# Two blocks on one core: the input's rows at 512 columns, and the working region 64 bytes further on

## What is computed

```python
x = first_block(x, meta_tokens, ...)     # 16 meta tokens ahead of the 512: 528 rows, dropped again at its end
    # h += W_out(recurrent heads + latent attention), squared-ReLU MLP of 4096
    # then a causal pooling layer and a second such MLP
return second_block(x, mem_2, ...)       # 512 rows
    # u = rms_norm(h); u @ gdn_w_in; gated delta rule, attention over 256 memory rows; @ w_out
    # f = swiglu(rms_norm(h), w_ffn_in, w_ffn_out), hidden width 2816
```

## Time and profile before

| | |
|---|---|
| time, median of three runs | 1871.85 us (1867.13 to 1872.07) |
| span of the profiled execution, first to last instruction | 1864.1 us |
| the profiled execution's own time | not given apart; one of the three |
| median less the span | 7.7 us |
| TensorE busy, mean granted clock | 1822.0 us (98%), 0.997 |
| VectorE, ScalarE busy | 1309.2 us (70%), 925.2 us (50%) |
| DMA | 162.55 MB, 87 GB/s |

### The profile page before, as it was taken

How to read it: one execution, slowest core, us unless ns; L and a number is a source line. 1 busy time by engine, 2 the same in 40 slices (tenths; PEclk the granted TensorE clock), 3 DMA queues, 4 the chain that set the end, 5 groups by cost and what they waited for, 6 DMA issues and landing times.

```text
span 1864.1 us, 31132 instructions
## 1 busy us (share of the span) xinstructions
PE 1822.0 (98%) x12498; PEld 1661.9 (89%) x12498; DVE 1309.2 (70%) x1882; ACT 925.2 (50%) x1557; POOL 33.4 (2%) x31
## 2 busy tenths in 40 slices
PE   7999999999999999999999999999999999999997
PEld 7888878999999999898899877787889898999996
DVE  4664476767777775877777768678738379877775
ACT  5456454544343446654344433645567464544453
POOL 0110001100000000000000000000000000000000
PEclk9999999999999999999999999999999999999999
DMA  5211101222233232333233322222200422333331
GB/s 197 70 57 58 60 1 46 81 102 91 91 106 99 80 119 91 102 102 103 91 111 103 103 92 91 80 68 79 80 1 27 144 80 91 114 102 102 107 109 57
DMA packets 63364, 162.55 MB, mean 87 GB/s; under 512 B 4632, under 2 KB 29464, under 8 KB 63096
## 3 DMA queue, kind: packets, MB, share of 16 engines
q1 hardware_dynamic: 62368, 158.59, 25.7%
q10 hardware_dynamic: 856, 2.00, 0.3%
HBM read 156.38 MB, written 4.19 MB: 86 GB/s over the span
## 4 chain that ended last, share of the span: by engine, by line
PE 89%; DVE 5%; ACT 3%; DMA 1%; issue 1%; DVEq 1%; ACTq 0%; SPq 0%
PE ps L714 76%; PE ps L1389 2%; DMA ULF<-W 1%; PE ps L929 1%; PE ps L1409 1%; PE ps L1258 1%; DVE wlo L3379 1%; PE ps L1394 0%; PE ps L1235 0%; PE ps L1237 0%; PE ps L904 0%; ACT WU L2620 0%; DVE wlo L3009 0%; PE ps L905 0%; PE ps L1521 0%
## 5 line engine op out<-in xcount | busy, mean ns | idle before, releaser
L714 PE MATMUL ps<-UH,whi 128*128 128x264 f32 (+2 forms) x1280 | 413.0, 323 | 11.2 <-DVE wlo L3009 10.4
L714 PE MATMUL ps<-UL,whi 128*128 128x264 f32 (+2 forms) x1280 | 403.0, 315 | 0.0
L714 PE MATMUL ps<-UH,wlo 128*128 128x264 f32 (+3 forms) x992 | 288.5, 291 | 0.0
L714 PEld LDWEIGHTS ps<-UH,whi 128*128 128x128 f32 x1280 | 241.4, 189 | 30.3 <-issue 13.6
L714 PEld LDWEIGHTS ps<-UL,whi 128*128 128x128 f32 x1280 | 241.4, 189 | 17.6 <-issue 2.4
L714 PEld LDWEIGHTS ps<-UH,wlo 128*128 128x128 f32 (+1 forms) x992 | 186.9, 188 | 2.7
L1947 ACT ACTIVATE whi<-raw 128x1024 fp32r<-128x1024 f32 x114 | 119.3, 1052 | 83.9 <-PE ps L714 63.2
L714 PE MATMUL ps<-KFH,whi 128*128 128x264 f32 x512 | 145.7, 285 | 1.6 <-DVE KFL L3421 1.5
L714 PE MATMUL ps<-KFH,wlo 128*128 128x264 f32 x512 | 145.3, 284 | 0.0
L714 PE MATMUL ps<-KFL,whi 128*128 128x264 f32 x512 | 145.2, 284 | 0.0
L714 PE MATMUL ps<-TH,whi 128*128 128x256 f32 x504 | 139.1, 276 | 0.0
(11 more groups left out here) (577 smaller groups left out, 4552.8 us busy)
## 6 DMA issues: line engine op xcount, KB each, us to landing
raw<-W SPq DMA_DIRECT2D x134, 512.0 KB, 3.5
raw_p<-W SPq DMA_DIRECT2D x46, 1024.0 KB, 4.9
ULF<-W SPq DMA_DIRECT2D x44, 512.0 KB, 4.0
raw_d<-W SPq DMA_DIRECT2D x14, 512.0 KB, 3.9
H<-xT SPq DMA_DIRECT2D x4, 528.0 KB, 7.5
spill<-H SPq DMA_DIRECT2D x1, 2048.0 KB, 7.0
H<-spill SPq DMA_DIRECT2D x1, 2048.0 KB, 8.4
MEM<-memT ACTq DMA_DIRECT2D x1, 1024.0 KB, 4.8
```

What stands on the lines that cost most here:

```text
L714: mm = pe.matmul(dst, a, b, start=start and n == 0, stop=stop_ and n == 2, skip_group_check=again)
```

## The change

Two things move, and no instruction is added, removed or reordered, nor any wait.

- The stages that use 512 tokens get an input of their own, USH and USL, [128, 8, 512] each, placed inside UH's and UL's room at u_at + 384 = 82944, which is 81 x 1024. USL lies 16384 bytes behind USH. Every row of both begins at 0 modulo 1024. The DMA target for the second MLP's down pieces and the place of its snapshots are cut out of the same room with rows of 2048 bytes instead of 2112.
- S0 moves from 134080 to 134144, which is 131 x 1024; the rows that began at 960 modulo 1024 begin at 0. The first MLP's KFH and KFL move by 64 bytes too. OMH, MH, ML, KTH, KTL, the first MLP's UH and UL, and the weights stay.

```diff
@@ -177,7 +177,8 @@  (Space)
-    parts: list
+    inputs: object
+    inputs_lo: object
@@ -292,6 +293,8 @@  (build)
         UH = place("UH", [P, KT, L], FR)
         UL = place("UL", [P, KT, L], FR)
+        us_at = u_at + 384
+        assert us_at + 2 * KT * SEQ * 4 <= u_at + 2 * KT * L * 4
@@ -303,7 +306,7 @@
-        S0 = base[0]
+        S0 = base[0] + 64
@@ -443,12 +446,14 @@
+        USH, USL = region(us_at, ("USH", [P, KT, SEQ], FR), ("USL", [P, KT, SEQ], FR))
+        USF, USLF = region(us_at, ("USF", [P, KT, SEQ], F32), ("USLF", [P, KT, SEQ], F32))
...
         space0 = Space(L, HALF, [KFH0, KFH1], [KFL0, KFL1], [KG_0, KG_1], KTH, KTL, KX, KFO, UF[:, 0:4, HALF:L],
-                       ULF[:, 0:4, HALF:HALF + 2 * P], [slice(0, HALF), slice(HALF, L)], R2[:, :], R[1][:, :], ((7, 5, 6), (4, 5, 6)))
-        space1 = Space(SEQ, NMEM, [MFH0, MFH1], [MFL0, MFL1], [GM0, GM1], MTH, MTL, XT, FOM, UF[:, 0:4, META + NMEM:L],
-                       ULF[:, 0:4, META + NMEM:L], [slice(META, META + NMEM), slice(META + NMEM, L)], R2[:, META:L], R[1][:, META:L],
+                       ULF[:, 0:4, HALF:HALF + 2 * P], UH, UL, R2[:, :], R[1][:, :], ((7, 5, 6), (4, 5, 6)))
+        space1 = Space(SEQ, NMEM, [MFH0, MFH1], [MFL0, MFL1], [GM0, GM1], MTH, MTL, XT, FOM, USF[:, 0:4, NMEM:SEQ],
+                       USLF[:, 0:4, NMEM:SEQ], USH, USL, R2[:, META:L], R[1][:, META:L],
                        ((7, 1, 3), (4, 5, 6)))
@@ perceptron, mlp_pair
-                    return UH[:, k, h.parts[0]]
+                    return h.inputs[:, k, 0:h.half]
...
-                    half_product(z, v + 2, 1, lambda k: UH[:, 4 + k, h.parts[1]], lambda k: UL[:, 4 + k, h.parts[1]], False)
+                    half_product(z, v + 2, 1, lambda k: h.inputs[:, 4 + k, h.half:h.tokens],
+                                 lambda k: h.inputs_lo[:, 4 + k, h.half:h.tokens], False)
...
-                    tile(KT, h.tokens, lambda k: u(order[k]), lambda k: ul(order[k]), before=split_input(m) if j == 0 else None)
+                    tile(KT, h.tokens, lambda k: h.inputs[:, order[k], :], lambda k: h.inputs_lo[:, order[k], :],
+                         before=split_input(m) if j == 0 else None)
@@ the gate columns and the 36 gin tiles
-                mm = passes(ps[0:16, 7, :], ABH[:, k, :], ABL[:, k, :], tok(u(k), SEQ), tok(ul(k), SEQ), k == 0,
+                mm = passes(ps[0:16, 7, :], ABH[:, k, :], ABL[:, k, :], us(k), usl(k), k == 0,
...
-                tile(KT, SEQ, u, ul, before=between(j))
+                tile(KT, SEQ, us, usl, before=between(j))
@@ the first tiles of the last MLP, in halves and whole
-                        mm = passes(ps[:, 2 * (t % 2) + e // 2, x * NMEM:(x + 1) * NMEM], wh, wl, UH[:, k, part(x)],
-                                    UL[:, k, part(x)], k == 0, k == KT - 1)
+                        mm = passes(ps[:, 2 * (t % 2) + e // 2, x * NMEM:(x + 1) * NMEM], wh, wl, us(k)[:, half(x)],
+                                    usl(k)[:, half(x)], k == 0, k == KT - 1)
...
-                    mm = passes(ps[:, bank, :], wh, wl, UH[:, k, META:L], UL[:, k, META:L], k == 0, k == KT - 1)
+                    mm = passes(ps[:, bank, :], wh, wl, us(k), usl(k), k == 0, k == KT - 1)
@@ hi (ScalarE); lo (VectorE), input_hi and input_lo likewise
-                c = META if m >= 3 else 0
-                act.activation(UH[:, k, c:L], H[:, k, c:L], ACT.Copy, scale=g).then_inc(uh_done, 1)
+                if m >= 3:
+                    act.activation(USH[:, k, :], H[:, k, META:L], ACT.Copy, scale=g).then_inc(uh_done, 1)
+                else:
+                    act.activation(UH[:, k, :], H[:, k, :], ACT.Copy, scale=g).then_inc(uh_done, 1)
```

More of the change, by code:

```diff
@@ L531, in part, with half @@
             return slice(META + x * NMEM, META + (x + 1) * NMEM)
+        def half(x):
+            return slice(x * NMEM, (x + 1) * NMEM)
         def evacuated(t):
@@ L763, in ul, with us, usl @@
                 return UL[:, k, :]
+            def us(k):
+                return USH[:, k, :]
+            def usl(k):
+                return USL[:, k, :]
             def memory_sum():
@@ L822, in early_tokens @@
                 def early_tokens(k):
-                    return UH[:, k, h.parts[0]]
+                    return h.inputs[:, k, 0:h.half]
                 def early_tokens_lo(k):
-                    return UL[:, k, h.parts[0]]
+                    return h.inputs_lo[:, k, 0:h.half]
                 def mlp_pair(i):
@@ L2821, in input_hi @@
                     v = VEC["pre_ffn"] + k
-                    act.activation(UH[:, k, part(x)], H[:, k, part(x)], ACT.Copy, scale=vecs[:, v:v + 1]).then_inc(uh_done, 1)
+                    act.activation(USH[:, k, half(x)], H[:, k, part(x)], ACT.Copy, scale=vecs[:, v:v + 1]).then_inc(uh_done, 1)
             def input_squares(x):
@@ L2979, in lo @@
                 dve.wait_ge(uh_done, 8 * (m - (m > 5)) + (k if at is None else at) + 1)
-                c = META if m >= 3 else 0
-                dve.scalar_tensor_tensor(UL[:, k, c:L], H[:, k, c:L], g, UH[:, k, c:L].bitcast(F32), ALU.mult,
-                                         ALU.subtract).then_inc(u_done, 1)
+                if m >= 3:
+                    dve.scalar_tensor_tensor(USL[:, k, :], H[:, k, META:L], g, USH[:, k, :].bitcast(F32), ALU.mult,
+                                             ALU.subtract).then_inc(u_done, 1)
+                else:
+                    dve.scalar_tensor_tensor(UL[:, k, :], H[:, k, :], g, UH[:, k, :].bitcast(F32), ALU.mult,
+                                             ALU.subtract).then_inc(u_done, 1)
             def added(m, k):
@@ L3922, in input_lo @@
                     dve.wait_ge(uh_done, 40 + 8 * x + k + 1)
-                    dve.scalar_tensor_tensor(UL[:, k, part(x)], H[:, k, part(x)], vecs[:, v:v + 1],
-                                             UH[:, k, part(x)].bitcast(F32), ALU.mult, ALU.subtract).then_inc(u_done, 1)
+                    dve.scalar_tensor_tensor(USL[:, k, half(x)], H[:, k, part(x)], vecs[:, v:v + 1],
+                                             USH[:, k, half(x)].bitcast(F32), ALU.mult, ALU.subtract).then_inc(u_done, 1)
             def input_sum(x):
```

## The result

The changed kernel took 1879.72 us (median of 8 runs, 1878.5 to 1882.5), the kernel before beside it 1871.77 us (median of 8, 1864.16 to 1876.66): ratio 1.0051, 95% interval 1.0037 to 1.0066. It is slower, where 1868.6 us, no change, had been forecast. The profiled execution spans 1877.2 us, where that of before spans 1864.1, so the two traces differ by 13.1 us and the medians by 8.0. That the two numbers differ turned out to be part of the answer (experiments 8 to 10). Of the 7.7 us between median and span before, 2.0 are no more than what lies between an execution's time and its span (1879.16 and 1877.2 us for the changed kernel's profiled one); by that the profiled execution of before took about 1866.1 us, an estimate; that is none of the three times listed, and a quick one.

A forecast was written before the change was run, and what follows sets the result against it. TensorE, busy 98% of the span, was taken to bound the kernel by its matmul pace. With -3.2 us from USH and USL and nothing elsewhere, 1871.85 became 1868.6 us, read as the same; range 1858 to 1883.

The forecast's parts named there:

- (c): First MLP, 2 x 264 columns: a shift by 64 only permutes its rows of 2112 bytes; effect 0.
- (d): ScalarE and VectorE writes and the DMA go to other addresses, equally often, hidden by TensorE; nothing new is late.
- Step (a): USH and USL: 1080 matmuls of 512 columns go from 232.0 to MFH's 229.0 ns; 3.2 us less.
- Step (b): Working region starting at 0 instead of 960: no change, for 1356 matmuls of 512 columns and those of 256.
- 0 is the poor start: Working region's products slow to UH's pace at 0, TH to 117.9 ns; 1882.9 us, chance 0.17.
- 113.3 is no property of a start at 960: Last MLP: TH at 113.3 and MTH at 117.9 ns both start at 960, so TH could go to 117.9.
- Aligned is the quick state: 256-column products: 1560 matmuls gain 4.6 ns, 7.2 us, on top of 3.2; 1861.4 us, chance 0.29.
- clean reads: All fp32r products reach the plain products' pace, 215 ns for 512 columns; 1827.3 us, chance 0.07.
- Addresses don't matter: The 3 ns between UH and MFH come from something else that stays; 1871.9 us, the same, chance 0.10.
- nothing for the 696 products of the input with 256 columns: Input's 256-column matmuls: nothing put down, with 0 to 2.1 us of gain kept as bounds.
- The two rules set against each other: Operand reads: 16-byte lines would mean no effect of either part; the gap rule gives 216 ns for 512 columns.

The follow-up runs named there:

- experiment 8: Two kernels: 512-column rows at distance 0 from weights, TH, TL, MTH, MTL at 112, 1862.52 us; changed kernel with TH, TL 16 bytes back, 1872.07 us.
- experiment 9: Kernel before with TH and TL 48 bytes further on and FH, FL and XQ 192 further: 1865.23 us, ratio 0.9966.
- experiment 1: TensorE alone, 92 streams of 48 matmuls varying the starts of moving rows and weights and the high-to-low distance: 512 columns took 226.7 to 233.3 ns.
- experiment 3: Kernel before with the input's rows of 512 columns starting at 960 modulo 1024 and S0 unmoved: 1867.23 us, ratio 0.9985.
- experiment 4: Changed kernel with weights also 64 bytes further on, so moving rows keep the earlier distance from them: 1864.26 us, ratio 0.9985 to the kernel before.
- Experiments 5 and 10: TensorE-alone streams in 16-byte steps and with 0 to 3 matmuls ahead, 113.3 or 117.8 ns; kernel before unchanged, twice more, 1871.55 and 1868.86 us.
- experiment 2: Kernel before with only S0 moved 64 bytes further on: 1880.43 us, ratio 1.0060.

## Why the prediction was wrong

**What bounds the kernel: right.** A change of pace went to the end one to one (13.0 us of start-to-start time, 13.1 us of span), no wait of note was added, and the first 780 us stayed as they were but for the clock. Steps (c) and (d), both nothing, held nearly: the 4296 products of 264 columns took 531.5 us from start to start before and 532.2 after, VectorE and ScalarE are unchanged.

**Step (a), 3.2 us for USH and USL: failed.** After the change "high, low and all k start alike modulo 1024, as MFH and MFL do, so I take their pace". That they start alike is not what gives 229 ns; D = 64 does, and the changed rows are at D = 128. They came out at 232.0 to 232.6, the very pace of D = 128 in experiment 1. At D = 64 they have 228.9 (experiment 3) and 229.2 (experiment 4). The mixed rows of before average what their four D give, (228.9 + 232.4 + 233.3 + 226.7) / 4 = 230.3, a little under the 232.0 seen; the rest was not looked into.

**Step (b), nothing for the working region: failed, and here the time went.** The step had the right row in hand, UH at 0 with its 233 ns, beside 229 at 960, and read it as "a start at 0 by itself bought nothing", while it put the row's own pace nowhere into the sum. As the nearest row at 0 it was a price: 232.7 ns for MFH, FH and YH, 1356 matmuls. Measured, their paces cost 1.6 + 2.2 + 0.3 = 4.1 us, the 4.1 of the rival *0 is the poor start*; TH and TL gave 8.6 against its 7.0, since at D = 128 they run at 119.0 on average, a little slower than MTH had. The other products of 256 columns (the input, MTH, YH) added 1.6 us that it had left out, and part (a) brought nothing, as it said. That rival is what happened. Its 11.1 us stand against 13.0 between the traces, 14.5 without the half clock of before. Its time, 1882.9 us, came near the measured 1879.7 in part by luck: it priced too little and added it to a median that held most of TH's loss already. The range up to 1883 held the result because of this rival, not by the forecast's own steps. The rival's mechanism, the distance from the weights, is shown by experiments 1 and 4: at starts of 0 and D = 64 the loss is gone. Its chance in the prediction, 0.17, was too low because the step's test of it was "does 0 gain?", never "does 0 lose?".

**TH's 113.3 ns.** "113.3 is no property of a start at 960, since both start there" was right and stopped one question short. Experiments 5 and 10 show two lasting paces at D = 64, 113.3 and 117.8, from what ran just before in the one and from one execution to the next in the other; the trace that was read happened to be a quick one, which is why its span and the median stood 7.7 us apart, more than in other kernels here (changed kernel: 2.5). Of the 13.1 us between the traces 6.8 are TH's own spread (4.5 ns x 1512) that slower executions of before have already paid. The medians' 8.0 us is smaller for that reason, as far as the runs show; that most executions behind the median had TH slow is read from their times and from one trace of three, not from a trace of each.

**The other rivals.** *Aligned is the quick state* and *clean reads* fell: MTH at 118.1, USH of 256 columns at about 119, nothing near 215. *Addresses don't matter* fell with experiment 2. One more term was mis-sized: nothing for the 696 products of the input with 256 columns, with a gain of up to 2.1 us as its bound, where they lost 0.7.

**The two rules set against each other.** A shift of 16 bytes (experiment 8, second kernel) leaves every start a multiple of 16 and changes TH's pace from 119.0 to 113.3 ns. The Trainium skill, "SBUF — State Buffer", section Door 1: The DMA port swizzle, has lines of 16 bytes and by it both placements would read alike; for these reads the measurement differs and decides. The shortest pace that any distance gave for 512 columns is 226.7 ns. The Trainium skill, "TensorE: Matmul & The Clock Gate", section Back-to-back issue gap, gives 216 ns as the gap of a matmul by itself, and about 131 ns for a stream that loads weights for each matmul. The prediction took only the first; no fp32r stream here, with new weights for every matmul, came to either.

## What to carry to other kernels

Where TensorE streams fp32r products back to back with new weights each time, the moving row's start has to be judged against the weights' start, modulo 256 bytes, and not against a round number: here 512-column rows are best at a distance of 0 (226.7 ns in every stream of TensorE alone, up to 236.7 elsewhere), 256-column rows at 112 (113.3, up to 120.0 elsewhere). A pace read from one trace can be one of two states of the same code; before it is used in a sum, read it in a second execution, and take a gap between span and median that is larger than usual as a warning. Look for short falls of the granted clock before two traces are compared: a mean of 1.00 over some hundred us hides them. Of the kernels tried, the one with both distances chosen has the lowest time and beats the kernel before by 0.18% (1862.5 us against 1865.2, interval 0.07% to 0.30%), measured where the kernel before was mostly quick; that of experiment 9 beat it by 0.34% where it was mostly slow. The first of the two is also steadier: 1861.3 to 1864.6 us, where the kernel before beside it ranges over 11 us.

## What the runs showed of the hardware that was not expected

- The pace of back-to-back matmuls depends on the distance between the two operands' starts modulo 256 bytes, in steps as fine as 16: 226.7 to 236.7 ns for 512 columns, 113.3 to 120.0 for 256, with every other engine idle (fp32r, weights loaded for every matmul). In steps of 64 bytes the starts themselves didn't matter, nor did the distance from high to low rows in steps of 256. Why the distance matters no run shows.
- Some distances have two lasting paces for the same instructions: 256 columns at D = 64 have 113.3 or 117.8 ns, and two matmuls of 256 columns ahead of 24 others are enough to choose. 512 columns at D = 64 have 228.9 or, in two streams, 233.3; at D = 240 mostly 233.3 or 236.7, twice 226.7.
- The two paces appear from one execution of a program to the next (TH at 113.3 in two traces of the kernel before, at 117.8 in a third). What in such executions chooses TH's pace was not found.
- In the middle of the work the granted clock falls to half, 1.2 GHz, for 3.4 us in some executions and not in others of the same program: none, one and three times in the three traces of the kernel before. Each fall that could be compared cost 1.5 to 1.7 us.
- Rows of 1056 bytes, whose D changes from row to row, have one pace, 120.8 to 120.9 ns for 264 columns, wherever they begin.
